# Attended values in quarter arrays with the scaling of probabilities on ScalarE, and VectorE's convolution taps ahead of the weight remainders, in a hybrid attention and SSD layer on one core

## The reference

```
xn = rmsnorm(h, norm1_w);  proj = xn @ w_in
q, k, v, z, xbc, dt_raw, ga_raw, gs_raw = split(proj)
attn  = banded_sink_attention(q, k, v, sinks) @ w_attn_o
xbc   = silu(causal_dwconv(xbc, ssd_conv_w, ssd_conv_b))     # 4 taps
xs, bm, cm = split(xbc)
y     = ssd_chunked(xs, softplus(dt_raw + dt_bias), a_log, bm, cm, d_skip) * silu(z)
h     = h + (sigmoid(ga_raw + ba) * attn + sigmoid(gs_raw + bs) * (groupnorm(y) @ w_ssd_o)) @ w_out
... then rmsnorm, w_up, 3-tap conv, silu gate, w_down, final rmsnorm
# attention, per block of 128 queries, over the own and the previous block (window 128):
scores = q @ k.T / 8, masked;  m = max(scores.max(), sink)
p = exp(scores - m);  probs = p / (p.sum() + exp(sink - m));  out = probs @ v
```

## Time and profile before

| | |
|---|---|
| median of 3 runs | 1030.26 us (1030.12 to 1030.32) |
| the profiled execution, its time | 1030.5 us |
| its span | 1028.8 us |
| PE busy | 1019.6 us, 99% |
| PEld, DVE, ACT, POOL busy | 832.2, 642.0, 457.5, 69.4 us |
| granted TensorE clock | 0.999 |
| chain that ended last | PE 89%, DVE 8%, ACT 2%, issue 1% |

### The profile page before, as it was taken

How to read it: one execution, slowest core, us unless ns; L and a number is a source line. 1 busy time by engine, 2 the same in 40 slices (tenths; PEclk the granted TensorE clock), 3 DMA queues, 4 the chain that set the end, 5 groups by cost and what they waited for, 6 DMA issues and landing times.

```text
span 1028.8 us, 13393 instructions
## 1 busy us (share of the span) xinstructions
PE 1019.6 (99%) x5095; PEld 832.2 (81%) x5095; DVE 642.0 (62%) x909; ACT 457.5 (44%) x818; POOL 69.4 (7%) x112
## 2 busy tenths in 40 slices
PE   9999999999999999999999999999999999999997
PEld 8887777777788888888888888898888888888886
DVE  7636999794476685985754544666666676641323
ACT  6344555454555545765533222544444444331233
POOL 0000000000231120122220100000000000000000
PEclk9999999999999999999999999999999999999999
DMA  7622221225556424445362743223232223332322
GB/s 219 123 85 82 83 62 63 83 83 120 159 133 162 133 72 137 140 127 153 100 205 82 266 143 108 77 82 113 91 122 82 82 85 119 93 128 87 95 69 82
DMA packets 123498, 116.48 MB, mean 113 GB/s; under 512 B 21342, under 2 KB 111782, under 8 KB 123447
## 3 DMA queue, kind: packets, MB, share of 16 engines
q1 hardware_dynamic: 95509, 94.74, 29.9%
q10 hardware_dynamic: 25346, 12.59, 5.2%
q0 software_dynamic: 2592, 8.46, 2.2%
HBM read 109.41 MB, written 6.36 MB: 113 GB/s over the span
## 4 chain that ended last, share of the span: by engine, by line
PE 89%; DVE 8%; ACT 2%; issue 1%; DMA 0%; SPq 0%; ACTq 0%; DVEq 0%
PE banks L1259 27%; PE banks L1260 27%; PE banks L1261 27%; DVE conv_acc L1207 3%; PE banks L1363 1%; DVE w_lo L856 1%; PE banks L1356 1%; PE banks L1331 1%; PE banks L1351 1%; PE banks L1339 1%; DMA w_raw<-in_w_in 0%; ACT probs L614 0%; PE banks L1321 0%; PE banks L1311 0%; ACT w_hi L576 0%
## 5 line engine op out<-in xcount | busy, mean ns | idle before, releaser
L856 DVE TENSOR_TENSOR w_lo<-w_raw,w_hi 128x1024 fp32r<-128x1024 f32 (+1 forms) x166 | 198.3, 1234 | 123.7 <-ACT w_hi L576 122.4
L576 ACT ACTIVATE w_hi<-w_raw 128x1024 fp32r<-128x1024 f32 (+1 forms) x166 | 164.1, 1037 | 109.2 <-PE banks L1261 107.9
L1259 PE MATMUL banks<-xn_hi,w_hi 128*128 128x512 f32 x528 | 211.5, 401 | 0.0
L1260 PE MATMUL banks<-xn_lo,w_hi 128*128 128x512 f32 x528 | 206.1, 390 | 0.0
L1261 PE MATMUL banks<-xn_hi,w_lo 128*128 128x512 f32 x528 | 206.0, 390 | 0.0
L1259 PE MATMUL banks<-hn_hi,w_hi 128*128 128x512 f32 (+1 forms) x376 | 141.3, 376 | 0.0
L1260 PE MATMUL banks<-hn_lo,w_hi 128*128 128x512 f32 (+1 forms) x376 | 141.2, 375 | 0.0
L1261 PE MATMUL banks<-hn_hi,w_lo 128*128 128x512 f32 (+1 forms) x376 | 141.2, 375 | 0.0
L1259 PEld LDWEIGHTS banks<-xn_hi,w_hi 128*128 128x128 f32 x528 | 99.1, 188 | 28.2 <-issue 8.5
L1261 PEld LDWEIGHTS banks<-xn_hi,w_lo 128*128 128x128 f32 x528 | 99.1, 188 | 21.4
L1260 PEld LDWEIGHTS banks<-xn_lo,w_hi 128*128 128x128 f32 x528 | 99.3, 188 | 19.0
(11 more groups left out here) (221 smaller groups left out, 1429.8 us busy)
## 6 DMA issues: line engine op xcount, KB each, us to landing
w_raw<-in_w_in SPq DMA_DIRECT2D x29, 1024.0 KB, 5.4
w_raw<-in_w_up SPq DMA_DIRECT2D x22, 1024.0 KB, 5.0
decay<-acs_scratch ACTq DMA_DIRECT2D x16, 512.0 KB, 5.9
w_raw<-in_w_ssd_o SPq DMA_DIRECT2D x8, 1024.0 KB, 5.3
w_raw<-in_w_down SPq DMA_DIRECT2D x8, 1024.0 KB, 5.0
w_raw<-in_w_in SPq DMA_DIRECT2D x16, 256.0 KB, 4.5
w_raw<-in_w_attn_o SPq DMA_DIRECT2D x16, 256.0 KB, 4.7
decay_off<-acs_scratch ACTq DMA_DIRECT2D x32, 128.0 KB, 3.6
```

The lines of the kernel that those rows point to most:

```text
L576: A.activation(whi[:, c % 2, lo_:hi_], raw[:, c % 2, lo_:hi_], ACT.Copy).then_inc(w_rounded, 1)
L856: V.tensor_tensor(wlo[:, c % 2, lo_:hi_], raw[:, c % 2, lo_:hi_], f32(whi[:, c % 2, lo_:hi_]), ALU.subtract).then_inc(w_split, 1)
L1259: T.matmul(out_, w[0], m[0], start=first, stop=False)
L1260: T.matmul(out_, w[0], m[1], start=False, stop=False)
```

## The change

1. **Values by quarters.** The keys and queries of a block are each cut in halves of 64. The parts above or below the band are left out where they are all masked. For a step pair with a previous block, 12 matmuls of 64 x 64 weights and 256 columns replace 4 of 128 x 64 weights and 512 columns; without one, 8 replace 2. The keys' first half goes to bank 2, the second to bank 7. ACT copies bank 2 into a new tile `attended` (`attended_left`), DVE adds bank 7 to it (`attended_sum`), and `a_hi` and `a_lo` are made from the sum.
2. **Scaling on ACT.** DVE keeps the sum and the reciprocal (`denominators`); the scaling of `probs` is four ACT instructions of 128x128 (`probabilities`).
3. **Slots.** Transposes and values ride one PE slot (half a unit) later, `attended_hi` and `attended_lo` two ACT and DVE slots later, and the starts of the steps (ATT_AT) are shifted by up to half a unit. The first decay load of the SSD rides one slot later.
4. **Order on DVE in a bc or xs unit.** The taps come first; then, in unit a, the first half of `w_lo` for the next chunk, slots 0 and 1, and the second half; then the multiplication. Before, both halves of `w_lo` stood at the head of the chunk and slot 0 before the taps.

```diff
-    ("PE", "scores", 1), ("PE", "probs_t", 5), ("PE", "values", 7), ("ACT", "own_scores", 1),
-    ("ACT", "exponentials", 4), ("ACT", "attended_hi", 10),
-    ("DVE", "mask_and_max", 1), ("DVE", "probabilities", 4), ("DVE", "probs_t_masked", 7),
-    ("DVE", "attended_lo", 10))
+    ("PE", "scores", 1), ("PE", "probs_t", 6), ("PE", "values", 8), ("ACT", "own_scores", 1),
+    ("ACT", "exponentials", 4), ("ACT", "probabilities", 5), ("ACT", "attended_left", 11), ("ACT", "attended_hi", 12),
+    ("DVE", "mask_and_max", 1), ("DVE", "denominators", 4), ("DVE", "probs_t_masked", 8),
+    ("DVE", "attended_sum", 11), ("DVE", "attended_lo", 12))
...
-ATT_AT = (-4.5, -3.25, -2, -0.5, 1, 2.75, 4.5, 6.25, 8, 9.75, 11.5, 13, 14.25, 15.5, 16.75, 18)
+ATT_AT = (-4.5, -3.25, -2, -0.75, 0.75, 2.5, 4.25, 6, 7.75, 9.25, 11, 12.5, 13.75, 15, 16.25, 17.5)
...
+        if _n == 0 and _w == "load_decay":
+            _v = -6
...
+                    elif what == "attended_left":
+                        if n % 2:
+                            eng.wait_ge(a_pv, n // 2 + 1)
+                            A.activation(att[:, :, :, :].rearrange("p h j q -> p (h j q)"), PS[:, 2, :],
+                                         ACT.Copy).then_inc(a_left, 1)
+                    elif what == "probabilities":
+                        eng.wait_ge(a_rd, n + 1)
+                        for j in range(GQ):
+                            ins = A.activation(Pr[:, n % 2, j, :], Pr[:, n % 2, j, :], ACT.Identity,
+                                               scale=rden[:, n % 2, j:j + 1])
+                        ins.then_inc(a_pr, 1)
...
-                        eng.wait_ge(a_pv, n // 2 + 1)
+                        eng.wait_ge(a_sum, n // 2 + 1)
...
-                        eng.wait_ge(a_rd, n + 1)
-                        V.tensor_tensor(Pr[:, k, :, :], Pr[:, k, :, :], bcast(rden[:, k, :], GQ, P),
-                                        ALU.mult).then_inc(a_pr, 1)
...
+                    elif what == "attended_sum":
+                        if n % 2:
+                            eng.wait_ge(a_left, n // 2 + 1)
+                            av = att[:, :, :, :].rearrange("p h j q -> p (h j q)")
+                            V.tensor_tensor(av, av, PS[:, 7, :], ALU.add).then_inc(a_sum, 1)
...
-                elif 1 < c + 1 < len(CHUNKS) and c not in (AT[("out", 3)], AT[("up", 0)]):
+                elif 1 < c + 1 < len(CHUNKS) and c not in (AT[("out", 3)], AT[("up", 0)]) and kind not in ("bc", "xs"):
                     split(c + 1)
...
-                    rides(c, u, 0)
                     if kind not in ("bc", "xs"):
+                        rides(c, u, 0)
                         rides(c, u, 1)
...
+                        if u == 0:
+                            split(c + 1, part=(0,))
+                        rides(c, u, 0)
                         rides(c, u, 1)
+                        if u == 0:
+                            split(c + 1, part=(1,))
                         eng.wait_ge(c_tanh, k_conv + 1)
...
-                        take(7, a_ol, n // 2 + 1)
-                        for back in (1, 0) if b_ else (0,):
+                        take(2, a_left, n // 2 + 1)
+                        take(7, a_sum, n // 2 + 1)
+                        def part(keys, queries, back, start, stop):
+                            for hh in range(2):
+                                ks, qs = slice(keys * HD, keys * HD + HD), slice(queries * HD, queries * HD + HD)
+                                probs = ptp_of[hh][ks, :, qs] if back else ptc[ks, hh, :, qs]
+                                ins = T.matmul(PS[hh * HD:(hh + 1) * HD, (2, 7)[keys],
+                                                  queries * GQ * HD:(queries + 1) * GQ * HD]
+                                               .rearrange("p (j q) -> p j q", j=GQ),
+                                               v[ks, b_ - back, (g + hh) * HD:(g + hh + 1) * HD],
+                                               probs, start=start, stop=stop)
+                            return ins
+                        if b_:
+                            part(0, 0, 1, True, False)
+                            part(1, 1, 1, True, False)
+                            part(0, 0, 0, False, True)
+                            part(1, 1, 0, False, True)
+                            part(0, 1, 0, True, True)
+                            ins = part(1, 0, 1, True, True)
```

More of the change, by code:

```diff
@@ L215, in hybrid_layer @@
         Pr = sb("probs", [P, 2, GQ, P], 132)
+        att = sb("attended", [P, 2, GQ, HD], 136)
         ptc = sb("probs_t_cur", [P, 2, GQ, P], 138)
@@ L850, in bcast, with split @@
                 return cols.unsqueeze(2).broadcast_to([P, n, width])
-            def split(c, pairs=0):
-                for k, (lo_, hi_) in enumerate(halves(c)):
+            def split(c, pairs=0, part=(0, 1)):
+                for k in part:
+                    lo_, hi_ = halves(c)[k]
                     eng.wait_ge(w_rounded, 4 * pairs + (2 * c + k + 1))
@@ L939, in rides @@
                         V.tensor_tensor(es[:, k, :], snk_, m_[:, k, :], ALU.subtract).then_inc(a_df, 1)
-                    elif what == "probabilities":
+                    elif what == "denominators":
                         k = n % 2
@@ L966, in rides @@
                         eng.wait_ge(a_oh, n // 2 + 1)
-                        V.tensor_tensor(a_lo[:, tl, tok], PS[:, 7, :].rearrange("p (j q) -> p j q", j=GQ),
-                                        f32(a_hi[:, tl, tok]), ALU.subtract).then_inc(a_ol, 1)
+                        V.tensor_tensor(a_lo[:, tl, tok].rearrange("p j (h q) -> p h j q", h=2), att[:, :, :, :],
+                                        f32(a_hi[:, tl, tok]).rearrange("p j (h q) -> p h j q", h=2),
+                                        ALU.subtract).then_inc(a_ol, 1)
                     elif what == "x_dt":
@@ L1325, in rides @@
                         eng.wait_ge(a_ptm, n + 1)
-                        take(7, a_ol, n // 2 + 1)
-                        for back in (1, 0) if b_ else (0,):
+                        take(2, a_left, n // 2 + 1)
+                        take(7, a_sum, n // 2 + 1)
+                        def part(keys, queries, back, start, stop):
                             for hh in range(2):
-                                rows = slice(hh * HD, (hh + 1) * HD)
-                                probs = ptp_of[hh][:, :, :] if back else ptc[:, hh, :, :]
-                                ins = T.matmul(PS[rows, 7, :], v[:, b_ - back, (g + hh) * HD:(g + hh + 1) * HD],
-                                               probs.rearrange("p j q -> p (j q)"), start=back == 1 or b_ == 0,
-                                               stop=back == 0)
+                                ks, qs = slice(keys * HD, keys * HD + HD), slice(queries * HD, queries * HD + HD)
[13 more added lines that the diff above has]
+                            ins = part(1, 0, 1, True, True)
+                        else:
+                            part(0, 0, 0, True, True)
+                            part(1, 1, 0, True, True)
+                            part(0, 1, 0, True, True)
+                            ins = part(1, 0, 0, True, True)
                         ins.then_inc(a_pv, 1)
```

5 lines of the change are left out of this document (3 added, 2 removed).

## The result

| | before | after |
|---|---|---|
| median | 1030.29 us (4 runs) | 1049.07 us (4 runs, 1048.87 to 1050.7) |
| ratio | 1 | 1.0185, interval [1.0168, 1.0203] |
| profiled execution, its span | 1030.5, 1028.8 us | 1048.95, 1047.2 us |
| granted TensorE clock | 0.999 | 0.996 |

The change makes the kernel 18.8 us slower. The forecast was 1044.5 us in a range of 1032 to 1052.

What follows compares the result with a forecast made beforehand. PE's own work, 99% busy, was taken to bound the kernel, with DVE nearly full. Terms -2.5 - 0.8 + 15.4 + 2.5 - 0.3 = +14.3 us gave 1044.8 profiled, 1044.5 us by median; range 1032 to 1052 (forecast's own 1038 to 1052).

Steps and rivals of the forecast that it cites:

- The values: PE's value matmuls by quarters, four side by side: 0.41 us saved in each of six pairs, 2.5 us.
- The stalls in the attention: PE waits in bc1 to z2b for late `w_lo`, transposes, scaling and banks: 15.4 us together.
- the walk: Hand tracing of the PE, DVE and ACT queues from bc0a on, giving each stall; some forty links, about 0.1 us each.
- the sentence on the SSD: xs4, xs5 and xs7: slot 0 has no pieces, so no wait; the 0.3 us wait of L1351 goes.
- the 2.5 that I had: xs6a: the product with `decay` stands behind late taps and half of `w_lo`, so PE stalls 2.5 us.
- The sum: Whole kernel: all terms give +14.3 us on the profiled 1030.5, 1044.8 us, or 1044.5 by the median.
- Signs named ahead: New PE wait rows; taps' idle time some 12 us or more; wrong if bc3a starts within 1 us of before.
- Slack swallows the shifts: Rival, 14%: ACT work ends earlier than walked; only two attention chunks and xs6 stall, 1034 us.
- no change: Rival, 5%: the attention saves 3.3 us, xs6 and one chunk give it back, 1030 us.
- Quarters two at a time: Rival, 4%: value quarters run in twos, six pairs cost 1.0 us more each instead of 0.4 less, 1053 us.
- Faster: Rival, 9%: taps first bring tanh, rounding and bias early enough that no `w_lo` is late, 1027 us.
- the prediction's other figure: Scaling on ACT: the Trainium skill page's estimate of 1.6 us for four instructions, beside the row's 1.2.

Runs made afterwards that it cites:

- values_only: The kernel before with quarter values, copy and sum; scaling stays on DVE, `attended_hi`, `attended_lo` and first decay load one slot later: 1033.59 us, ratio 1.0031.
- bias_first: order_first with ACT's queue turned in unit a of bc0 to xs3: bias, then next chunk's rounding, slots 0 and 1, tanh: 1030.77 us, ratio 1.0001.
- order_back: The changed kernel with DVE's old order in all bc and xs units; quarter values, scaling on ACT and slots stay: 1032.71 us, ratio 1.0022.
- order_alone: The kernel before with only DVE's new order in the bc and xs units: 1055.16 us, ratio 1.0235.
- rides_first: The changed kernel with slot 0 back ahead of the taps, `w_lo` still behind them: 1044.94 us, ratio 1.0142.
- order_first: The changed kernel with DVE's new order kept in bc0 to xs3 and the old order back in xs4 to xs7: 1044.3 us, ratio 1.0127.
- scaling_only: order_back with whole values again, no copy or sum, `attended_hi` and `attended_lo` one slot earlier than in after; scaling on ACT: 1030.87 us, ratio 1.0005.
- remainders_first: The changed kernel with both halves of `w_lo` back at the chunk's head, slot 0 still behind the taps: 1035.35 us, ratio 1.0047.
- mixed: remainders_first with slot 0 behind the taps in the attention alone, ahead of them in xs4 to xs7: 1033.74 us, ratio 1.0032.
- late_left: mixed with the values' copy, sum, rounding and remainder one slot later, the last step's transposes half a unit later: 1035.64 us, ratio 1.0056.
- bias_first_2: bias_first with step 7's masked transposes two DVE slots earlier and, in xs2, ACT's slot 0 ahead of the next chunk's rounding: 1029.87 us, ratio 0.9994.

## Why the prediction was right, and where it was not

**The values**, -2.5 us: right to the hundredth on PE, 0.41 a pair, four quarters side by side. What it did not price is what the sum costs DVE by itself: values_only is about 3 us slower with DVE's old order.

**The stalls in the attention**, +15.4 us. Unit z3b, right behind the last rides of the attention, starts on PE at 256.48 (244.90 before): 11.6 later, where the walk had 12.1 (15.4 - 2.5 - 0.8). Read from the gaps between weight loads of after, less what the same pieces leave where nothing waits, place by place:

| place | walk | measured |
|---|---|---|
| transposes at the end of bc1b | 0.7 | 0.36 |
| bc3a start, middle (`w_lo`) | 1.8, 0.2 | 2.03, 0.26 |
| values 5 | 1.5 | 1.08 |
| xs0a start, middle (`w_lo`) | 0.55, 0.4 | 0.88, 0.91 |
| xs0b (its bank) | 1.4 | 1.39 |
| xs1a start (`w_lo`) | 2.4 | 2.53 |
| xs1a middle (values 7) | 2.1 | 0.60, and 1.1 of slower matmuls before it |
| z0 start (`w_lo`), end of xs2a, xs3 | 0.4, 0.45, 0.4 | 0.59, 0.1, 0.56 |
| z2 start (`w_lo`), z2b (bank 1) | 0.8, 2.3 | 0.97, 2.19 |
| sum | 15.4 | 14.5 + 1.1 |

The single errors are up to 0.5 us and in part cancel, as the prediction said they would. The one real difference is in xs1a. The walk let PE come to values 7 on time and wait 2.1 us; in fact PE came late, because its clock had fallen, and waited at most 0.6. The delay stands in the sum either way.

The walk's total is close in part by luck. Read by the same gaps, before's own waits in the attention were 1.3 us and not 0.8 (2.66, 2.60 and 2.04 us in bc2b, at xs0b and in z0b, where such pieces alone leave 2.44, 2.0 and 1.56). The gaps also make each of the five waits without a piece between the loads about 0.1 too long, since the load behind it follows after 0.11 us instead of 0.23. With both, 15.6 - 2.5 - 1.3 - 0.6 = 11.2 us, which is 0.4 short of the 11.6 measured.

**The step that failed** is the sentence on the SSD: "In xs4, xs5 and xs7 the pieces in slot 0 are none, and I find no wait", together with the one before it, "The 0.3 us wait of L1351 goes." From z3b to unit z7a after lost another 6.9 us (18.5 - 11.6), where I had 2.2. I looked for pieces of slot 0 and forgot that `w_lo` itself had moved in those chunks too. Four things were missing, 4.6 us together:
- 1.1 us at the start of z4a. DVE's and PE's timelines of after:

```profile
398.04 2.32 DVE L1226 SCALAR_TENSOR_TENSOR conv_acc<-banks,half_conv,conv_acc 128x511 f32<-128x511 f32 x3 [1.27 <-ACT conv_acc L787]
400.27 2.35 DVE L872 TENSOR_TENSOR w_lo<-w_raw,w_hi 128x1024 fp32r<-128x1024 f32 x2
```

```profile
401.63 0.47 PE L1283 MATMUL banks<-xn_hi,w_hi 128*128 128x512 f32 x1 [1.02 <-DVE w_lo L872]
```

- 0.4 us in the middle of z6a, where PE waits for the second half of `w_lo` (it ends at 460.2, PE loads at 460.26).
- 1.5 us at the end of z6a, where `xdt_decayed` comes behind that half, a multiplication and the taps. The wait of 0.3 us that the sum took away stood at this very place and grew to 1.5 instead. DVE, then PE, in after, and PE in before:

```profile
458.99 1.22 DVE L872 TENSOR_TENSOR w_lo<-w_raw,w_hi 128x1024 fp32r<-128x1024 f32 x1
...
461.27 2.30 DVE L1226 SCALAR_TENSOR_TENSOR conv_acc<-banks,half_conv,conv_acc 128x511 f32<-128x511 f32 x3
```

```profile
464.82 1.13 PE L1394 MATMUL banks<-xdt_decayed,b_nat_cb 128*128 128x512 f32 x2 [1.53 <-DVE xdt_decayed L997]
```

```profile
446.34 1.12 PE L1351 MATMUL banks<-xdt_decayed,b_nat_cb 128*128 128x512 f32 x2 [0.33 <-DVE xdt_decayed L978]
```

- 1.6 us in xs6 on top of the 2.5 that I had. The 2.5 itself came out (against the earlier trace rows), 2.45 us in PE's timeline of after:

```profile
436.41 1.39 PE L1406 MATMUL banks<-decay,xdt 128*64 128x128 f32 x16 [2.45 <-DVE decay L1002]
```

The matmuls behind it ran at the lower clock (below), which no walk over queues contains.

**The sum**, made against the profiled execution, gave 1044.8 us, and after's took 1048.95: 4.2 short, 4.7 too little in xs4 to z7 and 0.5 too much in the attention. (By the medians it is 1044.5 and 1049.07.) Nothing was lost elsewhere: bc0a starts 0.1 us later than before, z3b and xs4a are both 11.6 later, z7a and the unit 11 behind it both 18.5.

**Signs named ahead.** bc3a starts 1.9 us later than before; the prediction would have been wrong with less than 1. DVE's idle time ahead of the taps is 34.5 us, where "some 12 or more" was the sign; I set that bound too low by a factor of almost three, since I counted only the places that stall PE. All four rows of PE's waits that were named are there.

**The rivals.** "Slack swallows the shifts" and "no change" fall with bc3a and xs1a. "Quarters two at a time" falls with 0.41 saved a pair. "Faster" needed the last tap of bc1b within 3.4 us of bc2a's start; tanh, released by that tap, came at 120.89, 5.5 us behind the start at 115.39 (the walk: 5.2). Its idea was not wrong, though: bias_first shows that in the attention taps ahead of remainders need cost nothing once the bias is early (1030.77 us, against 1032.71 for order_back with the old order on both engines). What it got wrong is the engine whose order had to change.

## What to carry to other kernels

Before you put a piece that waits ahead of one that doesn't, look up who releases it and what stands in front of that in the releaser's queue: here one order on DVE made kernels 13.5 us apart, by whether ACT's bias came ahead of 3 us of ACT's own filler or behind it. A piece moved by a loop's code moves in every chunk that runs the loop, so walk through each kind of chunk and not only through those with rides. And a gain on a busy engine is worth what the consumers let through: 2.5 us less of matmuls cost one more sum a pair on a full DVE, and came out as a loss of about 3 us.

## What was not expected of the hardware

**After a longer stand PE's clock fell to half.** In after PE stood 2.2 us at the start of xs1a, worked for 1.0 us, and then the granted clock fell from 2.4 to 1.2 GHz (1.00 up to 164.0, 0.50 from there to about 167.4); the same after the 2.45 us at `decay` (0.50 from about 437.1 to 440.5). PE's timeline of after, and the stretches by window:

```profile
162.99 0.47 PE L1283 MATMUL banks<-xn_hi,w_hi 128*128 128x512 f32 x1 [2.18 <-DVE w_lo L872]
...
164.39 0.63 PE L1285 MATMUL banks<-xn_hi,w_lo 128*128 128x512 f32 x1
164.82 0.63 PE L1283 MATMUL banks<-xn_hi,w_hi 128*128 128x512 f32 x1
```

```profile
162.00:163.50 1.50, 0.51 (x2) 0.48 (x3) 1.50 (x2) 0.38 (x1) 0.00 (x0) 1.00 0.00 0
163.50:167.00 3.50, 3.50 (x11) 2.66 (x9) 3.40 (x8) 2.34 (x10) 0.00 (x0) 0.57 0.02 5
...
436.00:439.00 3.00, 2.59 (x22) 2.27 (x23) 3.00 (x5) 0.22 (x1) 0.00 (x0) 0.68 0.22 44
439.00:441.00 2.00, 2.00 (x9) 1.65 (x8) 1.85 (x4) 1.20 (x3) 0.00 (x0) 0.63 0.97 321
```

Matmuls of 512 columns start 0.43 us apart instead of 0.23 there. It cost after about 1.3 us in xs1 and 1.6 in xs6, together 2.9 of the 18.8 us. order_alone shows it longer, and there the clock fell at 126.7 while PE still stood (3.96 us, up to 128.16), and came back at 133.5:

```profile
124.00:128.50 4.50, 0.54 (x3) 0.35 (x3) 4.36 (x8) 0.63 (x1) 0.00 (x0) 0.80 0.01 2
128.50:135.30 6.80, 6.80 (x47) 4.89 (x46) 3.16 (x7) 0.60 (x1) 0.00 (x0) 0.63 0.50 154
```

order_back had one such fall, behind a stand of 2.74 us. Over all fourteen kernels, between 88 and 480 us, PE has twelve stands of 2 us or more in its timeline, and eleven have such a fall in their last part or within 1.5 us behind them; the twelfth, 2.09 us in order_alone at 241.3, has none. The stand of 1.9 us at the start of z2b went without one in after and in rides_first and was followed by one in order_first. In the eight kernels whose longest stands were under 1.8 us (before, scaling_only, remainders_first, mixed, late_left, values_only, bias_first and bias_first_2) no window of 2 us in that stretch shows a clock under 0.97. So the longest waits were mostly dearer here than their own length. That these stands caused the falls is read from their order in time in these traces; no run changed the length of one stand alone.

**Scaling on ACT.** Four 128x128 instructions took 1.26 us behind each other, as the earlier trace rows had it, also with a scale from another column each; the prediction's other figure, an estimate of 1.6 us for four, is not borne out.
